# Reordering ScalarE's copies in a hybrid mixer, and reciprocals through block transposition

## The reference

```python
# rms_norm: y = x * rsqrt(mean(x*x) + 1e-6) * w
h = h + 0.5 * swiglu(rms_norm(h, norm_ff1[i]), gate, up, down)
hn = rms_norm(h, norm_mix[i])
# layer 0:
z, xbc, dt_raw, gate_b, x_b = split(hn @ hyb_w_in)
y_a = ssd_mixer(z, xbc, dt_raw, ...)     # ends in rms_norm over two groups of 512 features
y_b = rglru_mixer(gate_b, x_b, ...)      # a recurrence over tokens, times gelu(gate)
h = h + concat([y_a, y_b]) @ hyb_w_out
# in rglru_mixer:
log_a = -8 * r_t * softplus(-lam)
a_t = exp(log_a)
mult = sqrt(-expm1(2 * log_a))
u = mult * (i_t * xb)
h_t = a_t * h_(t-1) + u_t
...
h = h + 0.5 * swiglu(rms_norm(h, norm_ff2[i]), gate, up, down)
```

## Time and profile before

| | |
|---|---|
| median of three runs | 1060.78 us (1060.72, 1060.78, 1062.34) |
| the profiled execution | 1062.19 us, of which the span is 1060.4 us |
| PE busy | 1048.1 us (99% of the span) |
| DVE busy | 794.6 us (75%) |
| ACT busy | 614.7 us (58%) |
| POOL busy | 51.0 us (5%) |
| mean granted PE clock | 0.996 of full speed |

### The profile page before, as it was taken

How to read it: one execution, slowest core, us unless ns; L and a number is a source line. 1 busy time by engine, 2 the same in 40 slices (tenths; PEclk the granted TensorE clock), 3 DMA queues, 4 the chain that set the end, 5 groups by cost and what they waited for, 6 DMA issues and landing times.

```text
span 1060.4 us, 18444 instructions
## 1 busy us (share of the span) xinstructions
PE 1048.1 (99%) x6654; PEld 942.4 (89%) x6654; DVE 794.6 (75%) x1137; ACT 614.7 (58%) x983; POOL 51.0 (5%) x70
## 2 busy tenths in 40 slices
PE   9999999999999999999999999999999999999997
PEld 8888888899998988888888888888999998888886
DVE  6888776679869978887756888775699578888653
ACT  6556555468878656565435656543556765656541
POOL 0200002100000000000111000011100000000011
PEclk9999999999999999999999999999999999999998
DMA  8866776549634756666755666676566446667671
GB/s 245 217 193 189 222 197 170 152 127 250 189 105 138 213 150 191 196 197 189 218 165 159 187 193 197 188 219 171 153 159 164 120 131 203 188 191 210 186 199 40
DMA packets 369283, 190.14 MB, mean 179 GB/s; under 512 B 5920, under 2 KB 368704, under 8 KB 369232
## 3 DMA queue, kind: packets, MB, share of 16 engines
q1 hardware_dynamic: 368976, 188.89, 63.0%
q0 software_dynamic: 256, 0.59, 0.3%
HBM read 187.86 MB, written 1.07 MB: 178 GB/s over the span
## 4 chain that ended last, share of the span: by engine, by line
PE 95%; DVE 2%; ACT 2%; issue 0%; DVEq 0%; ACTq 0%
PE psum L217 46%; PE psum L220 24%; PE psum L201 7%; PE psum L205 7%; PE psum L202 7%; PE psum L1923 1%; PE psum L1548 1%; DVE wlo L190 1%; PE psum L936 0%; ACT whi L185 0%; DVE arena L1204 0%; PE psum L953 0%; PE psum L880 0%; PE psum L954 0%; PE psum L1544 0%
## 5 line engine op out<-in xcount | busy, mean ns | idle before, releaser
L190 DVE TENSOR_TENSOR wlo<-raw,whi 128x1024 fp32r<-128x1024 f32 (+1 forms) x324 | 417.0, 1306 | 73.3 <-ACT whi L185 71.8
L185 ACT ACTIVATE whi<-raw 128x1024 fp32r<-128x1024 f32 (+1 forms) x324 | 354.0, 1113 | 27.7 <-PE psum L205 19.1
L217 PE MATMUL psum<-xn,whi 128*128 128x512 f32 x1408 | 354.5, 393 | 0.5 <-DVE xn L307 0.5
L217 PEld LDWEIGHTS psum<-xn,whi 128*128 128x128 f32 x1408 | 253.8, 189 | 46.3 <-issue 0.6
L220 PEld LDWEIGHTS psum<-xn,wlo 128*128 128x128 f32 x1408 | 192.5, 191 | 13.8
L220 PE MATMUL psum<-xn,wlo 128*128 128x256 f32 x1408 | 197.0, 283 | 0.0
L217 PE MATMUL psum<-hid,whi 128*128 128x512 f32 x704 | 171.8, 392 | 0.0
L217 PEld LDWEIGHTS psum<-hid,whi 128*128 128x128 f32 x704 | 128.2, 189 | 23.9
L201 PE MATMUL psum<-xn,whi 128*128 128x256 f32 x480 | 120.8, 290 | 0.3 <-ACT whi L185 0.3
L202 PE MATMUL psum<-xn,whi 128*128 128x256 f32 x480 | 117.6, 283 | 0.0
L510 ACT ACTIVATE arena<-arena 128x256 f32<-128x256 f32 x88 | 36.9, 419 | 110.5 <-DVE arena L574 110.4
(11 more groups left out here) (231 smaller groups left out, 879.5 us busy)
## 6 DMA issues: line engine op xcount, KB each, us to landing
raw<-in_ffn_gate SPq DMA_DIRECT2D x88, 512.0 KB, 3.9
raw<-in_ffn_up SPq DMA_DIRECT2D x88, 512.0 KB, 3.9
raw<-in_ffn_down SPq DMA_DIRECT2D x64, 704.0 KB, 4.7
raw<-in_hyb_w_in SPq DMA_DIRECT2D x36, 512.0 KB, 4.8
raw<-in_dif_w_qkv SPq DMA_DIRECT2D x24, 512.0 KB, 4.5
raw<-in_hyb_w_out SPq DMA_DIRECT2D x16, 512.0 KB, 4.2
raw<-in_dif_w_o SPq DMA_DIRECT2D x8, 512.0 KB, 4.0
hid<-cs_rows SPq DMA_DIRECT2D x4, 512.0 KB, 6.4
```

The costliest lines, as they stand in the source:

```text
L185: act.activation(whi[:, s, 0:k * P], raw[:, s, 0:k * P], ACT.Copy).then_inc(s_whi, 1)
L190: dve.tensor_tensor(wlo[:, s, 0:k * P], raw[:, s, 0:k * P], whi[:, s, 0:k * P].bitcast(F32), ALU.subtract).then_inc(s_wlo, 1)
L217: pe.matmul(acc, hi[:, j, :], x[:, t, :, :], start=start and j == 0, stop=False)
```

## The change

Two things are changed. First, the order of ACT's work in the hybrid phase: the four copies `y_hi(4)` to `y_hi(7)` come together in step 18, ahead of the exponentials `decay_of_lru(4)` to `(7)`, which go to step 19 behind the conversion of pair 19; the conversion of pair 20 follows them, then the four `tanh_of_lru` and `square_of_lru`. Second, `token_scale` (six times) and `y_rrms` (twice) no longer take a reciprocal of 128x256. A new function transposes the 128x256 tile in blocks of 32x32, which puts the 256 tokens on partitions with equal columns within each block, takes the reciprocal of one column of each block (128x8), and transposes that back, repeated over 32 columns. The three instructions wait for one another on a new semaphore `s_turn`.

```diff
@@ -137,6 +137,7 @@
         s_stat = sem("s_stat")
         s_rms = sem("s_rms")
         s_rb = sem("s_rb")
+        s_turn = sem("s_turn")
         s_gu = sem("s_gu")
         s_cor = sem("s_cor")
         s_gn = sem("s_gn")
@@ -421,9 +422,24 @@
                 act.wait_ge(s_rb, n)
             act.activation(rms[:], sums_bank(n), ACT.Sqrt, scale=1.0 / D, bias=eps[:, 0:1]).then_inc(s_rms, 1)
 
+        def blocks_of_32(v):
+            return v.rearrange("p (b t) -> p b t", t=32)
+
+        def reciprocal_of_rows(dve, src, dst, turned, few, semaphore):
+
+            base = turns[0]
+            turns[0] += 2
+            dve.transpose(turned, src).then_inc(s_turn, 1)
+            dve.wait_ge(s_turn, base + 1)
+            dve.reciprocal(few, blocks_of_32(turned)[:, :, 0]).then_inc(s_turn, 1)
+            dve.wait_ge(s_turn, base + 2)
+            dve.transpose(blocks_of_32(dst), few.unsqueeze(2).to_broadcast([P, few.shape[1], 32])).then_inc(semaphore, 1)
+
+        turns = [0]
+
         def token_scale(dve, n):
             dve.wait_ge(s_rms, n + 1)
-            dve.reciprocal(rb[:], rms[:]).then_inc(s_rb, 1)
+            reciprocal_of_rows(dve, rms[:], rb[:], rb[:], small[:, 150:158], s_rb)
             dve.wait_ge(s_rb, n + 1)
 
         def add_residual(dve, n, d, acc, scale):
@@ -1153,10 +1169,10 @@
             todo[16] += [lambda: convert_hi_half(17, 0), lambda: square_y(3), lambda: convert_hi_half(17, 1)]
             todo[17] += [lambda: group_rms(0), lambda: group_rms(1)] + [lambda t=t: y_hi(t) for t in range(4)]
             todo[17] += [lambda: convert_hi_half(18, 0), lambda: convert_hi_half(18, 1), lambda: mult_of_lru(0)]
-            todo[17] += [lambda t=t: decay_of_lru(t) for t in range(4, 8)]
-            for t in range(4, NL):
-                todo[18] += [lambda t=t: y_hi(t), lambda t=t: tanh_of_lru(t)]
-            todo[19] += [square_of_lru]
+            todo[18] += [lambda t=t: y_hi(t) for t in range(4, NL)]
+            todo[19] += [lambda t=t: decay_of_lru(t) for t in range(4, 8)]
+            todo[19] += [lambda: convert_hi_half(20, 0), lambda: convert_hi_half(20, 1)]
+            todo[19] += [lambda t=t: tanh_of_lru(t) for t in range(4, 8)] + [square_of_lru]
             todo[20] += [lambda k=k: gelu(k) for k in range(4)]
             todo[21] += [lambda: lru_hi(0), lambda: lru_hi(1), lambda: mult_of_lru(1)]
             todo[22] += [lambda: lru_hi(2), lambda: lru_hi(3)]
@@ -1164,7 +1180,7 @@
             for s in range(24):
                 if s == 1:
                     token_rms(act, n)
-                if s >= 2 and s not in (16, 17, 18):
+                if s >= 2 and s not in (16, 17, 18, 20):
                     convert_hi(act, p0 + s, DT)
                 for task in todo[s]:
                     task()
@@ -1336,7 +1352,7 @@
 
             def y_rrms(g):
                 dve.wait_ge(s_yrms, g + 1)
-                dve.reciprocal(ygr[:, g, :], ygr[:, g, :]).then_inc(s_yrb, 1)
+                reciprocal_of_rows(dve, ygr[:, g, :], ygr[:, g, :], sz[:, 2 + g, :], tok[:, 8 * g:8 * g + 8], s_yrb)
 
             def y_norm(t):
                 if t % 4 == 0:
```

## The result

The changed kernel takes **1064.19 us** (median of 8 runs, 1062.34 to 1064.98) against 1060.75 for the kernel before (8 runs, 1060.18 to 1062.34). The ratio is 1.0026, with a 95% interval of 1.0017 to 1.0036. That is a loss of 3.4 us in the medians; forecast were 1063.3 us and a range of 1061.0 to 1065.0. The profiled execution took 1063.53 us, 1061.7 of it the span. Lines of the changed kernel are one higher than before up to the new function and 16 higher behind it: `y_lo` is L1367, `y_norm` L1361, `y_hi` L1150, `lru_lo` L1350, the root `mult_of_lru` L1118, the matmuls L202, L203 and L206.

A forecast was written before the change was run, and what follows sets the result against it. PE, busy 99% of the span, was taken to bound the kernel. 1062.19 - 4.45 (old loss) + 1.36 (first stall) + 3.07 (second stall) = 1062.2 us; 1.1 for the clock fall made 1063.3, range 1061.0 to 1065.0.

The forecast's parts named there:

- (a): PE stalls on `lru_lo` at block 8 and the clock falls in or behind that stall: 1063.3 us, chance 0.48.
- What can be won: Output projection blocks 0 and 1 took 10.21 us and need 5.76; reordering can win at most 4.45 us.
- The reciprocals: Transposition, short reciprocal and transposition back on DVE take 1.12 us against 1.75, 0.63 less each.
- (d): Transpositions on DVE are dear, about 0.95 us each, three instructions with reciprocal 2.2 us: 1064.3 us, chance 0.12.
- (e): The reciprocal gets no faster, 1.75 us for the three instructions, and only the order acts: 1063.4 us, chance 0.05.
- the six at the phase starts: The `token_scale` reciprocals on DVE at phase starts: their gain is hidden, costed at nothing.
- The first stall: PE waits for `y_lo` tiles 5, 6 and 7 in block 0, 1.36 us in total after the change.
- The second stall: PE waits for `lru_lo` tile 12 at block 8, 2.77 us, then three times 0.10: 3.07 us.
- Two figures for the root: Start of `mult_of_lru` on ACT: 350.3 by adding moved work to the old chain, 350.06 by stepping through without rounding.
- The tightest place of the forecast: PE has `whi` of block 6 at 346.7 for a need at 347.25, 0.6 us of slack.
- The clock: A PE clock fall at the block 8 gap, likelier than before: 1.4 us less 0.3, so 1.1 us.
- (b): PE stalls on `lru_lo` at block 8 but the clock stays up: 1062.2 us, chance 0.25.

The follow-up runs named there:

- `token_scale` kernel: Kernel before, with the block-transposition reciprocal only in `token_scale` (six times): 1061.26 us against 1061.43 for the kernel before.
- filler profiles: Kernel before with 12 unused matmuls on PE in its gap at block 0: 1061.07 us against 1061.43 for the kernel before.
- order-only kernel: Changed kernel with the old 128x256 reciprocals put back, so only ACT's new order remains: 1065.14 us against 1062.12 for the kernel before.
- The changed kernel again: The changed kernel, nothing altered, measured a second time: 1064.05 us against 1061.84 for the kernel before.
- the kernel with the exponentials between and the old reciprocals: Changed kernel with the four exponentials ahead of and between the `y_hi` copies and the old 128x256 reciprocals: 1061.11 us against 1061.84 for the kernel before.

## Why the prediction was right, point by point

The rival that was held likeliest, (a), is what happened: the gain at block 0 is given back at block 8, with a clock fall on top. 1063.3 us was 0.9 under the measured median, which lies inside the range. Times below are given for the profiled execution, less the 0.70 us by which it came to block 0 sooner.

**What can be won.** 4.45 us at blocks 0 and 1 is right, but its split was wrong: forecast were 3.06 us of waits and 1.4 of clock, and the `token_scale` and filler profiles, which have the same waits and no fall, lose 3.42 and 3.43, so the clock is 1.03 to 1.04. Nor is the fall the whole price of the upper level, 1.5 us, as the prediction read it. The sum is untouched by this, as it takes out the 4.45 whole; the 1.1 us for the next fall rests on it. The inference that the median is an execution without the fall held for the three runs then known, but not in general: in 29 executions beside the order-only kernel 16 were with it, and their median is 1062.12. That is why the same kernel stands at 1060.75 in one set and at 1062.12 in another.

**The reciprocals.** 1.12 us forecast, 322.33 - 321.13 = 1.20 measured. The term that was a little small is the transposition: 0.42 assumed from the one-input pass of the earlier trace rows, 0.445 measured. The estimate from the Trainium skill, "VectorE: DVE Perf Modes", section "The three transpose paths", was 0.44 and 1.17, and these runs agree with it better than with the row that I took. The advice of the same page of the Trainium skill, in "Rules for kernel authors", to keep the number of chained operations small did not decide here: three instructions in a chain, with all their fixed parts, beat one by 0.55 us. Rivals (d), transpositions near 0.95 us, and (e), no gain in the reciprocals, are refuted by the 0.445 us and by the order-only kernel, which loses 2.50 us in blocks 0 and 1 against 1.35. Costing the six at the phase starts at nothing fits the `token_scale` kernel, within its interval.

**The first stall.** 1.36 us forecast, 1.35 measured. That it is so near is in part luck: the pieces were to be 0, 0.48, 0.49 and 0.39 us, and the trace has about 0, 0.36, 0.49 and 0.40, with 0.10 behind the last tile. `y_hi(7)` was to start at 332.60 - 0.70 = 331.90 and started at 331.75. Block 2 was won 3.08 us earlier by the forecast, and 4.45 - 1.35 = 3.10 by the trace. As the sum assumed, pieces so short did not bring the clock down: 1.00 from 334 to 342.

**The second stall.** The mechanism is as forecast, and the size is the first term that was off. PE wanted tile 12 at 355.89 - 0.70 = 355.19 by the forecast, at 355.2 by the trace. The tile was to come at 358.66 - 0.70 = 357.96 and came at 358.32, 0.36 late. Nearly all of this is the root: forecast at 350.06 - 0.70 = 349.36, measured at 349.68. The way on from the root was forecast as 8.60 us and took 8.64. Two figures for the root stood in the prediction: the plain sum of moved work on the old chain, 350.3 (here 349.6), and a finer one by stepping through with the rounding left out, 350.06. The sum was right and the stepping was 0.3 too early; the step that failed is the choice between them. (The sum too was helped: the chain started 0.14 us sooner than forecast, at 332.07, and took 17.61 us where 17.45 were added up.) The tightest place of the forecast held: PE has no wait on `whi`, so the 0.6 us of slack at block 6 were enough. With three times 0.10 us behind it the stall is 3.43 us, as the order-only kernel shows without a clock fall, where 3.07 were forecast.

**The clock.** Forecast as likelier than before, at 1.1 us. Seen in both profiles of the changed kernel; with 3.43 for the stall bare its price is 5.87 - 1.37 - 3.43 = 1.07 us in one and 6.28 - 1.35 - 3.43 = 1.50 in the other. So the term was right in one and 0.4 short in the other, and right by luck, since it was 1.4 less 0.3 and the 1.4 should have been 1.04. The prices differ by where the fall lies. At the low clock matmuls start every 0.21 us instead of every 0.12 (360.64, 360.85 in the first profile), so 3.4 us of it cost an estimated 3.4 x (1 - 0.12 / 0.21), near 1.5 us, if PE has work throughout. In the first profile the fall begins at 359.3, behind the wait and the small waits of the next tiles, and the price is that. In the other it begins at 358.7: 0.5 us of it lie in the wait, 0.3 in the small ones, and 1.0 are left by the same estimate. In the kernel before, too, part of the fall lies over the small waits of the last tiles. The fastest run of the change, 1062.34, stands where rival (b) puts an execution without a fall, 1062.2; no profile of that run shows it.

**The rest of the difference.** The terms as measured close the sum on the profiled execution of before. (That they close shows that nothing outside these places differs; it does not test the cause of each.) The changed kernel again: 1062.19 - 4.46 + 5.87 = 1063.60; block 0 comes 0.16 us later (328.76 against 328.60), the last four matmuls take 0.51 more, and that makes 1064.27, where 1064.29 was measured. The first profile: 1062.19 - 4.46 + 6.28 = 1064.01, less 0.70 ahead of block 0, and 0.17 more at the end, where its last four matmuls take 0.88 us:

```profile
1055.21 0.88 PE L415 MATMUL psum<-con,small 128*128 128x128 f32 x4 [0.55 <-DVE small L1972]
```

That is 1063.48 against 1063.53. The term at the end stood nowhere in the prediction. Whether it belongs to the change is open: the kernel with the exponentials between and the old reciprocals has it too, at 0.51 us, the order-only kernel as well, and the others profiled here have none of it, or 0.3 in the `token_scale` kernel, in one execution each.

**Chances.** The 0.50 for within 0.2% was held a little likelier than the 0.42 for slower, and by the medians the change is 0.26% slower, with an interval from 0.17%: a close case, as forecast. What I weighed too low is how surely the fall comes: I split (a) and (b) as 0.48 to 0.25, and by the times it came in nearly every run.

## What to carry to other kernels

Work that is moved behind a critical step has not gone: add its whole length, with its table load, to the engine's chain up to the next deadline, and compare that with the slack there (here the tile came 1.6 us later and was wanted 3.1 us sooner, and the slack was 1.6). Look for the idle pieces that the critical step itself leaves on that engine, and put the moved work into those, one instruction each: with the four exponentials behind the copies the kernel was 2.2 us slower than before or more, with one in each idle piece 1.9 us faster. A gap on PE can cost more than its length, because the clock may fall with it, so one long gap can be worth filling with matmuls even when nothing can be won from its length. A price read off the distance of two levels of time can hold more than the cause one has in mind: a profile of the same stretch without the fall gave the fall's price here.

## What the hardware showed that I had not expected

The clock does not answer to a gap in the same way each time. In the kernel before, the same 1.34 us gap at block 0, with its short ones behind, was followed by a fall in about half of the executions, going by their two levels of time: 10 of 21 in one set, 16 of 29 in another (in the set of 31 the levels touch, at 1061.84 and 1061.93). The `token_scale` profile shows such a gap, 1.36 us, with the clock at 1.00. In the order-only kernel's profile a gap of 2.96 us passed with the clock at 1.00, whereas in the changed kernel a gap of 2.95 us at the same place was followed by a fall, in one profile before the gap's end and in the other a microsecond behind it. Why is open; no run here tells it.

Matmuls that do no useful work, issued while PE would wait, kept the clock at 1.00 around the gap in the profile of both kernels that had them, and gave 1.17 us of the median back in the changed kernel. In the kernel before its median was 0.4 us lower with them, which the interval does not tell from nothing; there the fall came only half of the time.

An ACT instruction on 8 columns takes 0.20 us at its spacing, half of one on 256 columns (0.40), so with 32 times fewer columns it took half the time, and no less. I had expected 0.13.
